# Differential attention: scaling one probability block of a pair instead of two

## The reference, cut to what matters

```
s = jnp.einsum('bhcqd,bhckd->bhcqk', q_blk.astype(f32), kf)
s = jnp.where(k_pos[None, :] <= q_pos[:, None], s, -1e30)
prob = jax.nn.softmax(s, axis=-1)
attn = prob[:, :, 0] - lam * prob[:, :, 1]
return jnp.einsum('bhqk,bhkv->bhqv', attn, vf)
...
o = rms_norm(o, subln_g, SUBLN_EPS) * (1.0 - lam_init)
o = o.reshape(B, S, D).astype(xn.dtype) * jax.nn.silu(gate)
return o @ w_out
```

## Time and profile before

| | |
|---|---|
| three runs of the kernel | 1071.31, 1072.02, 1073.11 us; median 1072.02 |
| the profiled execution | 1073.78 us, of which the span is 1071.9 |
| TensorE busy | 1025.9 us, 96% (8490 matmuls) |
| weight loads (PEld) | 858.1 us, 80% |
| GpSimd busy | 753.5 us, 70% |
| ScalarE busy | 563.1 us, 53% |
| VectorE busy | 525.4 us, 49% |
| TensorE's granted clock, mean | 0.993 |

### The profile page before, as it was taken

One profiled execution on the slowest core, in us unless ns is written; L12 is line 12 of the kernel. 1 busy time (PEld: TensorE's weight loads), 2 busy tenths in 40 slices (PEclk: granted clock), 3 DMA queues, 4 the chain that ended last, 5 costly groups with the idle time before them and its releaser, 6 DMA issues.

```text
span 1071.9 us, 20199 instructions
## 1 busy us (share of the span) xinstructions
PE 1025.9 (96%) x8490; PEld 858.1 (80%) x8490; DVE 525.4 (49%) x674; ACT 563.1 (53%) x894; POOL 753.5 (70%) x476
## 2 busy tenths in 40 slices
PE   7999999999999999999999999999999799999896
PEld 6888889999979969999997456589986686777675
DVE  3125185333546866523445848544458446133454
ACT  6557365444446956444443435221335458468945
POOL 5986559988866789988984175540317966998783
PEclk9999999999999999999999999999999999999998
DMA  9762445555545654556557435400004643654241
GB/s 361 273 236 79 150 158 179 185 194 181 194 167 167 199 176 158 191 184 194 183 191 277 155 121 185 137 4 4 4 5 139 234 156 137 213 177 138 82 154 40
DMA packets 45930, 170.44 MB, mean 159 GB/s; under 512 B 5104, under 2 KB 5360, under 8 KB 45328
## 3 DMA queue, kind: packets, MB, share of 16 engines
q1 hardware_dynamic: 42464, 155.91, 43.3%
q0 software_dynamic: 3376, 13.24, 3.5%
HBM read 167.03 MB, written 2.10 MB: 158 GB/s over the span
## 4 chain that ended last, share of the span: by engine, by line
PE 78%; ACT 8%; DVE 6%; POOL 4%; issue 2%; DMA 1%; SPq 0%; DVEq 0%; ACTq 0%
PE psum L484 22%; PE psum L521 20%; PE psum L748 16%; PE psum L2355 5%; PE psum L496 5%; POOL ring_r L837 3%; ACT high_r L1016 2%; PE psum L289 1%; DMA h<-x 1%; PE psum L2059 1%; DVE small L1910 1%; PE psum L2421 1%; PE psum L2242 1%; ACT arena L999 1%; ACT arena L1063 0%
## 5 line engine op out<-in xcount | busy, mean ns | idle before, releaser
L837 POOL TENSOR_TENSOR ring_r<-ring,high_r 128x512 fp32r<-128x512 f32 (+1 forms) x374 | 649.3, 1764 | 145.8 <-ACT high_r L1016 134.7
L1016 ACT CAST high_r<-ring 128x1024 fp32r<-128x1024 f32 x250 | 257.6, 1050 | 179.7 <-DMA ring<-w 175.4
L521 PE MATMUL psum<-x_high,high_r 128*128 128x256 f32 x640 | 183.0, 286 | 2.8 <-DVE x_low L353 2.8
L521 PE MATMUL psum<-x_low,high_r 128*128 128x256 f32 x640 | 181.7, 284 | 0.0
L521 PE MATMUL psum<-x_high,ring_r 128*128 128x256 f32 x640 | 181.7, 284 | 0.0
L720 DVE TENSOR_TENSOR arena<-arena 128x512 f32<-128x512 f32 x32 | 58.0, 1813 | 162.4 <-ACT arena L696 162.3
L521 PEld LDWEIGHTS psum<-x_high,high_r 128*128 128x128 f32 x640 | 123.5, 193 | 4.1 <-issue 2.5
L521 PEld LDWEIGHTS psum<-x_low,high_r 128*128 128x128 f32 x640 | 123.5, 193 | 0.5
L521 PEld LDWEIGHTS psum<-x_high,ring_r 128*128 128x128 f32 x640 | 123.4, 193 | 0.0
L748 PE MATMUL psum<-high_r,zz_high 128*128 128x512 f32 x256 | 99.9, 390 | 1.4 <-DVE zz_low L727 1.4
L748 PE MATMUL psum<-ring_r,zz_high 128*128 128x512 f32 x256 | 99.8, 390 | 0.0
(11 more groups left out here) (367 smaller groups left out, 1867.9 us busy)
## 6 DMA issues: line engine op xcount, KB each, us to landing
ring<-w SPq DMA_DIRECT2D x284, 512.0 KB, 3.8
row<-rows POOLq DMA_DIRECT2D x14, 512.0 KB, 6.4
arena<-relt SPq DMA_DIRECT2D x2, 1536.0 KB, 14.0
arena<-w POOLq DMA_DIRECT2D x4, 512.0 KB, 8.5
h<-x SPq DMA_DIRECT2D x1, 1024.0 KB, 11.3
arena<-lora POOLq DMA_DIRECT2D x2, 512.0 KB, 7.4
kept<-arena POOLq DMA_DIRECT2D x1, 1024.0 KB, 4.4
embedded<-kept POOLq DMA_DIRECT2D x1, 1024.0 KB, 5.1
```

The source lines that it names most:

```text
L521: ins = nc.tensor.matmul(out, a, b, start=(k == 0 and q == 0), stop=(k == KT - 1 and q == 2))
L837: ins = nc.gpsimd.tensor_tensor(low(m)[:, part], raw(m)[:, part], read(high(m))[:, part], ALU.subtract)
L1016: nc.scalar.copy(high(m), raw(m)).then_inc(high_made, 1)
```

## The change

Only the second block of a pair is still scaled, by the ratio -lam * sum0 / sum1, so that the sum of the blocks is the wanted combination times sum0. The missing factor 1 / sum0 per token and head is applied at the head norm: its square in the variance (before 1e-5 is added) and itself in the factor with which the outputs are multiplied. The ratio is computed on VectorE, behind the reciprocal, for which the array now has room for all pairs; the wait for an older combine, which kept one of two small buffers free, is gone, and the wait for lam moves from ScalarE to VectorE. The product with -lam on ScalarE (L1418) and two of its four scalings (L1422) are gone.

```
-        rd = [little(4).rearrange("p (c t) -> p c t", c=2) for _ in range(2)]
+        rc = little(32).rearrange("p (h c t) -> p h c t", c=2, t=NT)
+        ratio = little(16).rearrange("p (h t) -> p h t", t=NT)
+        rc_sq = little(16).rearrange("p (t h) -> p t h", t=NT)
...
                     act.wait_ge(rd_ready, g + 1)
-                    if g == 0:
-                        act.wait_ge(lam_done, 1)
-                    r1 = rd[g % 2][:, 1, :]
-                    settle(nc.scalar.activation(r1, r1, ACT.Copy, scale=nlam))
-                    for c in range(2):
-                        buf = sd[:, (2 * g + c) % 4, :]
-                        for t, cut in ((1, slice(0, 256)), (0, slice(256, 384))):
-                            ins = nc.scalar.activation(buf[:, cut], buf[:, cut], ACT.Copy, scale=rd[g % 2][:, c, t:t + 1])
+                    buf = sd[:, (2 * g + 1) % 4, :]
+                    for t, cut in ((1, slice(0, 256)), (0, slice(256, 384))):
+                        ins = nc.scalar.activation(buf[:, cut], buf[:, cut], ACT.Copy, scale=ratio[:, g, t:t + 1])
                     ins.then_inc(b_scaled, 1)
...
-                nc.vector.tensor_scalar(vr_y[:, :, u], vr_y[:, :, u], 1.0 / P, 1e-5, ALU.mult, ALU.add).then_inc(o_var, 1)
+                settle(nc.vector.scalar_tensor_tensor(out=vr_y[:, :, u], in0=vr_y[:, :, u], scalar=1.0 / P, in1=rc_sq[:, :, u],
+                                                      op0=ALU.mult, op1=ALU.mult))
+                nc.vector.tensor_scalar(vr_y[:, :, u], vr_y[:, :, u], 1e-5, None, ALU.add).then_inc(o_var, 1)
...
                 settle(nc.vector.reciprocal(rs_y[:, :, u], rt_y[:, :, u]))
+                settle(nc.vector.tensor_tensor(rs_y[:, :, u], rs_y[:, :, u], rc[:, u, 0, :].rearrange("p h t -> p t h"), ALU.mult))
...
                     dve.wait_ge(exp_done, HEADS + 2 * g + 2)
-                    if g >= 2:
-                        dve.wait_ge(comb_ready, g - 1)
-                    nc.vector.reciprocal(rd[g % 2], sums[:, 2 * g:2 * g + 2, :]).then_inc(rd_ready, 1)
+                    settle(nc.vector.reciprocal(rc[:, g], sums[:, 2 * g:2 * g + 2, :]))
+                    if g == 0:
+                        dve.wait_ge(lam_done, 1)
+                    nc.vector.scalar_tensor_tensor(out=ratio[:, g, :], in0=sums[:, 2 * g, :], scalar=nlam, in1=rc[:, g, 1, :],
+                                                   op0=ALU.mult, op1=ALU.mult).then_inc(rd_ready, 1)
+                    if g % 4 == 3:
+                        first = rc[:, g - 3:g + 1, 0, :].rearrange("p h t -> p t h")
+                        settle(nc.vector.tensor_tensor(rc_sq[:, :, g - 3:g + 1], first, first, ALU.mult))
```

## The result

Twenty runs of each kernel: 1074.18 us (median; 1073.12 to 1076.31) against 1072.15 us (1070.51 to 1074.19) before. The ratio is 1.0019, with a 95% interval of 1.0012 to 1.0026: 2.0 us slower where 2.1 us faster were forecast.

The account below looks back on a forecast made before the run. In the second attention ScalarE's chain, from 983.73 us to the squares of 1013.64, was taken to bound the kernel. 3.3 us gained there less 1.2 in the tail gave 2.1, from 1072.02 to 1069.9 us, range 1068.2 to 1072.5.

Parts of the forecast that it names:

- the place: Second attention: ScalarE's savings count only from pair 4 (983.73 us) on; before 982 us TensorE sets the time.
- the cost per pair: ScalarE's scaling in pairs 4 to 7: 1.03 us removed per pair, the ratio ready 0.21 us later than the reciprocal was.
- the rule for the added operations: VectorE's added two-tensor operations: 0.17 us up to the rest of a GpSimd instruction, 1.29 (L837) or 2.4 us (gate rows).
- the loads of tables: ScalarE's table loads: they go ahead of their operation's wait, without waiting for TensorE.
- Pair 6: 1.03, in all 2.7 us.: ScalarE's scaling of pair 6: the full 1.03 us saved, 2.7 us early in all, GpSimd having just gone idle.
- So this tail is longer by 1.2 us.: Second half's head variance to gate: 5.35 us plus 0.3 of waiting instead of 4.45, so 1.2 us longer.
- The wait w: Second tail, before the first GpSimd end lets the added operation in: 0 to 1.3 us (2.4 behind gate rows), taken as 0.3.
- What follows 1020.44 us moves as a whole.: Transposes, output projection and last gates after the second attention: they shift together, so the 2.1 us gained stay.
- within 0.2%: Whole kernel: no change that a measurement can tell, the limit being about 2.1 us; chance 0.48.
- the cancelling rival: Pairs' gains and added waits cancel, w of 1.3 to 2.4 us in the tail: 0 to 1.1 us gained, 1071.4 us; 0.10.
- the variance behind the gate rows: First head variance misses its slot, L1990 waits 2.4 us behind GpSimd's L970: 0.5 us slower, 1072.5 us; chance 0.15.
- the starved one: An added operation on the chain loses several turns to GpSimd, five L837 instead of one: 3.3 us slower, 1075.3 us; 0.08.

Follow-up runs that it names:

- e6: Changed kernel with only the first half's norm freed of the added operations (1e-5 times sum0 squared in its variance); ratio 1.0018 to the kernel before.
- e3b: Changed kernel with the second half's small variance and reciprocal-root arrays in PSUM; 1069.25 us against 1072.22 for the kernel before, ratio 0.9972.
- e2: Changed kernel with 1e-5 times sum0 squared added in the variance and no added product at the norm, both halves; 1069.23 us, ratio 0.9971 to before.
- e11: The same kernel as e2 run once more, on another chip; 1070.07 us, ratio 0.9978 to the kernel before.
- e8: Changed kernel with 15 idle products on TensorE ahead of its wait for the second head gate; ratio 0.9995 to the kernel before.
- e4_nonorm: Changed kernel with the head norm of the kernel before, the factor 1/sum0 left out of the computation; ratio 0.9977 to the kernel before.
- e12_second_eps: Changed kernel with only the second half's norm freed of the added operations (1e-5 times sum0 squared in its variance); ratio 0.9980 to the kernel before.

## Why the prediction was wrong

Right were the place (ScalarE's chain from pair 4 on), the cost per pair, the rule for the added operations (a GpSimd instruction each when it runs without a gap), that L1989 would take over 1 us in both halves, and the loads of tables. Up to the first squares the sum holds. Counted from pair 1's scores, the exponential behind pair 4's scaling is 1.03 us early (0.9 forecast), the first squares 1.84 (1.7).

Three steps failed.

*"Pair 6: 1.03, in all 2.7 us."* The exponential behind it was 1.95 us early: the pair gave 0.1. I let the added product of the first norm end with the gate rows; it came 0.08 us after GpSimd had begun the next L839 and took 1.27 us, so the norm ended 0.5 us early instead of 1.4, and the ratio, behind it on VectorE, was late. e6 gives back 1.03 us at the squares. The step was taken as hidden, with the slack already used up by L1989; a second wait of the same kind had nothing in front of it. The squares came 2.57 us early, 3.3 forecast.

*"So this tail is longer by 1.2 us."* It was 2.7: mis-sized. The wait w, from the end of the sum (1011.33) to the first GpSimd end (1012.49), was 1.2 us instead of 0.3, since the variance arrived just after GpSimd had begun an L839 (1011.19), and the gate, which I let in at once, waited 1.0 too. Between them the added product came 0.3 us sooner than my 2.8 (2.5 after that first end). Both waits were inside the bounds I gave for single waits; I took favourable phases for both. e3b shows the small operations' share as GpSimd's; the gate's own wait stayed there (1.15 us).

*"What follows 1020.44 us moves as a whole."* It didn't: TensorE's idling of 3.4 us brought the clock down, 2.0 us. No rival had it. The forecast's own numbers gave only 1.1 us of idling (0.8 as before, and 0.3 more since TensorE's work came 2.4 us early and the gate 2.1); the rest, 2.3 us, is what the first two steps missed (2.1 early forecast, 0.15 late measured). So this step hung on the other two, and yet 1.1 us would not have been safe: in e2 and e11 0.9 went with a fallen clock. e8 shows its price, with the same late transposes. Without it the change would have been within 0.2% (0.15 us by the profile), a case that I gave 0.48.

The sum with the measured sizes: 2.57 - 2.72 - 2.0 = -2.15 us. Up to the transposes the cancelling rival, to which I gave 0.10, is nearest to what happened. The one slow rival with a mechanism near this, the variance behind the gate rows, did not occur (the scores of pair 7, heads 14 and 15, began 0.7 us early); the starved one neither: the ratio took 0.22 us in pairs 4 to 6 and 0.38 in pair 7, as expected.

The lock of the Trainium skill (SBUF — State Buffer, "SBUF: two separate sides") agrees with the three small operations of the second tail, whose ends lie 0.03 to 0.05 us behind GpSimd's. One of them, L1989, has a single SBUF input; that section gives the lock also to a VectorE operation in a 2-port performance mode, which the prediction left out, and no run here shows in which mode L1989 ran. The row that speaks against its "starts first" (L1910, 6.92 us) is there again in the kernel after, as L1907 with 6.95 us at 845.3; the runs did not explain it.

## What to carry to other kernels

Price a small VectorE operation with two SBUF inputs (here also a 128x8 tensor_scalar from SBUF to SBUF), in a serial stretch beside a busy GpSimd, at up to one GpSimd instruction, and at a whole one when it follows another such operation. Two added ones made the tail 2.7 us longer here (the three small operations took 3.1 us where one had taken 0.9, and the gate 0.4 more); with an operand in PSUM each of the three took 0.17 us. Before an operation is put on such a path, look for algebra that needs none (1e-5 times sum0 squared instead of two products). And add up TensorE's idle time ahead of a matmul stage, by the bad bounds of the forecast too: 3.4 us in one piece cost 2 us more through the clock.

## What the runs showed that was not expected

A fill of TensorE's wait with idle products brought the whole 2 us back only when it was complete: with 1.2 us of it left idle the clock was still lower for part of the next stage (7.33 us for L484). And idle time alone doesn't tell: with 0.9 us before the transposes and 1.06 behind them the clock fell in the profiles of e2_eps and e11_eps_again (7.33 and 7.32 us for L484), with 1.0 and 1.06 it did not in e4_nonorm, e3b_psum and e12_second_eps (5.68 to 5.71). TensorE in e2_eps, then in e4_nonorm:

```profile
1014.29 1.09 PE L228 MATMUL psum<-con,arena 128*128 128x128 f32 x8 [0.90 <-DVE arena L2005]
1016.44 0.48 PE L484 MATMUL psum<-high_r,x_high 128*128 128x512 f32 x1 [1.06 <-DVE x_low L349]
```

```profile
1014.07 1.09 PE L228 MATMUL psum<-con,arena 128*128 128x128 f32 x8 [0.99 <-DVE arena L2004]
1016.22 0.47 PE L484 MATMUL psum<-high_r,x_high 128*128 128x512 f32 x1 [1.06 <-DVE x_low L349]
```

The profiles of e4_nonorm, e3b_psum and e12_second_eps are each of the fastest run of their kernel (1067.50, 1068.88 and 1068.62 us, the medians 2.1, 0.4 and 0.8 us above), those of e2_eps and e11_eps_again of middling ones. So the difference may lie between executions and not between the kernels, and in those three "the clock stayed up" is shown for one run each. What decides is open; the spread of e11's runs, 1066.48 to 1071.14 us, may be the same thing.
